# Feed-forward stage: two weight chunks per turn, and later SBUF operands moved to a multiple of 64 bytes

## The reference, cut to what matters

```
# first block: sparse attention mixer (16 heads), then a gated feed-forward layer
h = x + nsa_mixer(rmsnorm(x)) ; h = h + swiglu(rmsnorm(h)) ; x = rmsnorm(h)
def swiglu(h, w_in, w_out):              # D_FF = 5632
    z = h @ w_in                         # 2048 -> 2 * 5632
    a, b = z[..., :D_FF], z[..., D_FF:]
    return (jax.nn.silu(a) * b) @ w_out  # 5632 -> 2048
# second block: mLSTM branch and pooling branch, gated merge, output projection
proj = h @ w_in_2 ; ... ; merged = sigmoid(g_a)*(y_a @ w_a) + sigmoid(g_b)*(y_b @ w_b)
x = x + rmsnorm(merged @ w_out_2)
```

## Time and profile before

| | us |
|---|---|
| median of 3 runs | 2156.36 (2156.34 to 2156.58) |
| the profiled execution | 2156.56 |
| its span | 2154.9 |
| PE busy in it | 2144.7 |
| DVE busy | 1402.0 |
| ACT busy | 1045.4 |

### The profile page before, as it was taken

The page is one execution under the profiler, slowest core; times in us unless marked ns, Lnnn a source line. Parts: engine busy times, 40 slices in busy tenths (PEclk is TensorE's granted clock), DMA queues, the critical chain, the costliest instruction groups (busy, mean ns, idle before and its releaser), DMA issues.

```text
span 2154.9 us, 34222 instructions
## 1 busy us (share of the span) xinstructions
PE 2144.7 (100%) x12210; PEld 1875.6 (87%) x12210; DVE 1402.0 (65%) x1840; ACT 1045.4 (49%) x1371; POOL 68.8 (3%) x145
## 2 busy tenths in 40 slices
PE   9999999999999999999999999999999999999998
PEld 8888889888888888888888888888888888888886
DVE  7766655766666666645556777867777676566564
ACT  6565555544444444434445555444454454444443
POOL 1001221000000000000000000000000000000000
PEclk9999999999999999999999999999999999999999
DMA  8585333555656566565555555545555555555554
GB/s 297 186 271 192 120 128 128 185 186 185 195 169 205 181 196 191 173 200 186 186 185 181 166 169 194 185 158 194 186 176 177 169 191 181 191 188 188 184 200 137
DMA packets 109319, 396.60 MB, mean 184 GB/s; under 512 B 12387, under 2 KB 12403, under 8 KB 109105
## 3 DMA queue, kind: packets, MB, share of 16 engines
q1 hardware_dynamic: 106848, 386.97, 55.3%
q0 software_dynamic: 2240, 8.38, 1.2%
q10 hardware_dynamic: 144, 0.03, 0.0%
HBM read 390.87 MB, written 2.13 MB: 182 GB/s over the span
## 4 chain that ended last, share of the span: by engine, by line
PE 99%; DMA 0%; ACT 0%; POOL 0%; POOLq 0%; issue 0%; SPq 0%
PE set L1534 51%; PE set L1542 26%; PE set L1560 4%; PE set L1566 2%; PE set L1506 2%; PE set L1505 2%; PE set L1504 2%; PE set L1490 1%; PE set L1492 1%; PE set L1491 1%; PE misc L1677 1%; PE set L1648 1%; PE misc L1750 1%; PE misc L1736 1%; PE misc L1897 0%; PE misc L1752 0%
## 5 line engine op out<-in xcount | busy, mean ns | idle before, releaser
L807 DVE TENSOR_TENSOR w_hl<-raw,w_hl 128x1024 fp32r<-128x1024 f32 x729 | 886.6, 1225 | 574.3 <-ACT w_hl L485 568.4
L485 ACT ACTIVATE w_hl<-raw 128x1024 fp32r<-128x1024 f32 x729 | 762.2, 1056 | 798.8 <-PE set L1542 354.7
L1534 PE MATMUL set<-x_hl,w_hl 128*128 128x512 f32 x3520 | 857.2, 393 | 0.0
L1534 PEld LDWEIGHTS set<-x_hl,w_hl 128*128 128x128 f32 x3520 | 644.5, 188 | 124.6 <-issue 0.7
L1542 PEld LDWEIGHTS set<-x_hl,w_hl 128*128 128x128 f32 x3520 | 452.9, 191 | 18.6 <-issue 0.9
L1542 PE MATMUL set<-x_hl,w_hl 128*128 128x256 f32 x3520 | 462.9, 283 | 0.0
L1534 PE MATMUL set<-f_hl,w_hl 128*128 128x512 f32 x704 | 172.7, 396 | 0.0
L1534 PEld LDWEIGHTS set<-f_hl,w_hl 128*128 128x128 f32 x704 | 129.3, 188 | 28.1
L492 ACT ACTIVATE cross<-set 128x512 f32<-128x512 f32 (+1 forms) x142 | 83.2, 586 | 124.2 <-PE set L1534 112.0
L1542 PEld LDWEIGHTS set<-f_hl,w_hl 128*128 128x128 f32 x704 | 90.1, 188 | 4.3
L1560 PE MATMUL set<-w_hl,x_hl 128*128 128x512 f32 x384 | 92.9, 391 | 0.0
(11 more groups left out here) (318 smaller groups left out, 1792.0 us busy)
## 6 DMA issues: line engine op xcount, KB each, us to landing
raw<-in_weights SPq DMA_DIRECT2D x730, 512.0 KB, 4.1
bias_g<-bias POOLq DMA_DIRECT2D x4, 572.0 KB, 3.9
cur<-in_cur POOLq DMA_DIRECT2D x4, 535.0 KB, 3.6
h<-in_x SPq DMA_DIRECT2D x4, 512.0 KB, 7.4
bias<-u_dram POOLq DMA_DIRECT2D x1, 2048.0 KB, 15.0
out<-y_t SPq DMA_DIRECT2D x8, 256.0 KB, 2.4
post_row<-in_post POOLq DMA_DIRECT2D x1, 1024.0 KB, 6.5
w<-in_w POOLq DMA_DIRECT2D x1, 256.0 KB, 4.8
```

The source lines that it names most:

```text
L485: a(high, whole, ACT.Copy).then_inc(hi_ready, 1)
L807: tt(low, whole, high.bitcast(F32), ALU.subtract).then_inc(lo_ready, 1)
L1534: last = mm(out[:, f * 2 * S:(f + 1) * 2 * S], w[:, 0, c], hl[:, kt, :, :], start=first and k == 0, stop=low_first, skip_group_check=True)
```

## The change

In the feed-forward stage (`up` and the down loop) `gemm` gets `paired=True`. The chunks of a unit then run two at a time (`two_chunks`): for the first pair both high groups and then both low groups, for the next pair both low groups and then both high groups, and so on. Of a unit of 11 the last chunk stands alone. `chunks_done` is counted after the second group of each chunk. The wait for `hi_ready` stands in front of every high group now, also in blocks that are not paired. The tensors `f_lead` and `ya_lead` are gone, and `o_lead` (32 bytes) stands ahead of `o_hl`: `o_hl` now starts at byte 180032, `f_hl` and `ya_hl` at 129536, `yb_hl` at 162304, `m_hl` at 178688, all multiples of 64 (and so do the activations and sums that follow them). `x_hl`, `w_hl`, `raw` and `blk_hl` stay where they were. The queues of DVE, ACT, POOL and SP have the same rows in the same order as before.

```diff
@@ sbuf
+            o_lead = sb("o_lead", [P, 8], scope=s1c)
             o_hl = sb("o_hl", [P, HEADS, 2, S], F32R, scope=s1c)
...
-        f_lead = sb("f_lead", [P, 8], scope=s2)
         f_hl = sb("f_hl", [P, FKT, 2, S], F32R, scope=s2)
...
-        ya_lead = sb("ya_lead", [P, 8], scope=s3)
         ya_hl = sb("ya_hl", [P, KT, 2, S], F32R, scope=s3)
...
@@ PE
+        def high_and_low(at, j, out, hl, kts, first, low_first):
...
             def high():
+                pe.wait_ge(hi_ready, at.at(j) + 1)
...
+            return (low, high) if low_first else (high, low)
+
+        def unit_features(at, j, out, hl, kts, first, low_first):
+
+            one, other = high_and_low(at, j, out, hl, kts, first, low_first)
+            one()
+            return other()
+
+        def two_chunks(at, js, k0, out, hl, ready, low_first):
+
+            parts = []
+            for n, j in enumerate(js):
+                kts = range(4 * (k0 + n), 4 * (k0 + n) + 4)
+                parts.append(high_and_low(at, j, out, hl, kts, k0 + n == 0, low_first))
+                if ready:
+                    pe.wait_ge(*ready(kts[-1]))
+                parts[-1][0]()
+            for one, other in parts:
+                other().then_inc(chunks_done, 1)
...
-        def unit(at, j0, number, the_set, n, ready, hl, emit, steps, first_wait=None):
+        def unit(at, j0, number, the_set, n, ready, hl, emit, steps, first_wait=None, paired=False):
...
+            if paired:
+                for j in range(0, n, 2):
+                    two_chunks(at, range(j0 + j, j0 + min(j + 2, n)), j, sets[the_set % 2], hl, ready, j % 4 == 2)
+                    for k in range(j0 + j, j0 + j + 2):
+                        if steps and k in steps:
+                            steps[k]()
+                return
...
@@ def up(i, first)
-                 steps={3: lambda: stats(0, 0, 5)} if first else None)
-            gemm(Pos(C_UP + NB, i, 2 * NB), i * 4 + (B_UP + 2), B_UP)
+                 steps={3: lambda: stats(0, 0, 5)} if first else None, paired=True)
+            gemm(Pos(C_UP + NB, i, 2 * NB), i * 4 + (B_UP + 2), B_UP, paired=True)
...
-                gemm(Pos(C_DOWN + b * ND, i, 2 * ND), i * 4 + (B_DOWN + 2 * b), B_DOWN, n=ND, hl=f_hl,
+                gemm(Pos(C_DOWN + b * ND, i, 2 * ND), i * 4 + (B_DOWN + 2 * b), B_DOWN, n=ND, hl=f_hl, paired=True,
```

More of the change, by code:

```diff
@@ L1523, in block_tokens_apart @@
             return last
-        def unit_features(at, j, out, hl, kts, first, low_first):
+        def high_and_low(at, j, out, hl, kts, first, low_first):
             w = w_hl[at.slot(j)]
@@ L1596, in gemm @@
         def gemm(at, number, the_set, n=NB, ready=None, hl=x_hl, emit=(unit_features, unit_features), steps=None,
-                 first_wait=None):
+                 first_wait=None, paired=False):
             for half in range(2):
                 unit(at, half * (n // 2), number + half, the_set + half, n // 2, ready if half == 0 else None, hl,
-                     emit[half], steps, first_wait if half == 0 else None)
+                     emit[half], steps, first_wait if half == 0 else None, paired)
         def narrow(at, out):
```

## The result

The changed kernel takes 2168.28 us (median of 5 runs, 2168.22 to 2168.47) against 2156.49 for the kernel before: ratio 1.0055, 95% interval 1.0044 to 1.0066, 11.8 us slower. The forecast was 2164.1. The measured time lies 1.3 us above the forecast's own range (2161.5 to 2167) and inside the range given for 8 in 10 (2157.5 to 2170). The profiled span is 2166.7.

What follows compares the result with a forecast made beforehand. PE bounds the kernel, busy throughout with 99% of the chain. Waits +16.0, turns -1.0 and addresses -7.3 sum to +7.7 us on 2156.56, giving 2164.1; own range 2161.5 to 2167, 8 in 10 2157.5 to 2170.

Steps and rivals of the forecast that it cites:

- The waits, +16.0: PE waits for chunk 3's low part: 11 places at 0.96 us, three between down blocks at 1.75; 16.0 us lost.
- T + 7.32: Behind a value block, DVE ends chunk 3's low part 7.32 us after PE starts the next block; PE wants it at 6.51.
- Rival B: Chunk 3's low part comes in time after all, so only the gains stay: -8.3, 2148.1 us; chance 0.06.
- D: Waits longer or more, also at gate-to-value places, or restarts costing 0.3: about +6, 2170 us; chance 0.09.
- the restart: Extra time of PE's matmuls after a wait: 0.05 to start plus 0.10 for the slower second matmul; 0.3 as upper bound.
- The turns, -1.0: Fewer low-to-high turns on PE in `up` and down: 66 saved at 0.015 us, 1.0 us gained.
- The addresses, -7.3: Moved tensors get x_hl's pace: 5.8 us from 152 chunks, 2.0 from m_hl, less 0.5 for narrow o_hl matmuls; 7.3 gained.
- rival A: Tensors' place or what reads beside them, not the address, sets the pace: +15.0, 2171.4 us; chance 0.10.
- Rival C: Aligned f_hl, ya_hl and m_hl run at the bare 0.213 us per 512 columns: 22 us more gained, 2142; chance 0.03.
- The rule on 16-byte lines: Skill page cited against the address gain: crossing 16-byte lines costs, so a 32-byte shift gains nothing and the sum is +15.0.

Runs made afterwards that it cites:

- order_alone: The changed kernel with the old addresses, so only the paired turn order differs from the kernel before: 2171.11 us against 2156.53, ratio 1.0067.
- early_chunk3: The whole change, with ACT and DVE making chunk 3's high and low parts before the work that follows a value or down block: 2153.13 us, ratio 0.9984 to before.
- addr_alone: The kernel before with the change's new addresses and the old order: 2153.18 us, ratio 0.9984.

## Why the prediction was right and where it was not

**The waits, +16.0.** Right in place, number and size, and not by luck: each figure was worked out and each was met. order_alone costs 14.6 where the forecast has 16.0 - 1.0 = 15.0. A gate block takes 23.20 and a value block 22.22, where 23.2 and 22.25 were forecast. The row of the kernel before that gave it is the low part's end at T + 7.32, which could be carried over since nothing between the block end and that part was touched. early_chunk3 took exactly these waits away and 15.2 us with them. Rival B (the part comes in time) is out, and so is D (more or longer waits): no wait shows in value blocks, and the restart cost 0.10, not 0.3.

**The turns, -1.0.** Right in size for x_hl: `up` of early_chunk3 is 490.11 where addr_alone, like before, has 490.77, so 0.7 for 44 turns, and runs of 32 wide matmuls take the 7.28 forecast. Not in down: there the paired order has 247.90 and addr_alone 247.31, 0.6 more rather than 0.3 less. In the trace of early_chunk3 both kinds of f_hl are a little slower than in addr_alone, 233.1 / 119.0 against 232.7 / 118.6, and steps of 229 and 237 ns follow each other in the long runs; why the order does this at that distance is not shown. With the old addresses it did not: the order cost down 253.97 - 248.28 = 5.7 us there and 253.79 - 247.31 = 6.5 with the new ones. These 0.8 cover the 0.6 that is left of the 11.8 when 14.6 and -3.35 are added, 11.2.

**The addresses, -7.3.** This is the term that was mis-sized: -3.35 measured. The step that failed is "I take 7.3 because x_hl is the only aligned tensor in the same role". Alignment to 64 was one of several things in which x_hl differed, and the one that counts is that x_hl and w_hl start at the same place modulo 256, while f_hl moved from 160 to 128 away. One sample of an aligned tensor could not tell these apart, as the prediction said under rival A. The pieces: f_hl 1.0 instead of 3.4; ya_hl 4 x 0.09 = 0.4 instead of 1.2; yb_hl 0.2 instead of 0.6; m_hl 0.1 (its stage is 92.79 us instead of 92.86) and not 2.0. And the o_hl stage, booked as 0.6 for its 16 feature chunks less 0.5 for 384 narrow matmuls, gained 1.5: its narrow pace is 113.7 instead of 118.5, since o_hl came to 192 modulo 256 from w_hl. So 1.5 of the 3.35 came from where the prediction booked nearly nothing, and that part of the gain was luck. Rival A ("the place of the tensors or what reads beside them") was nearer to the cause, but not with its price of nothing. Its full form gave 2171.4; the measured 2168.28 lies between it and the forecast. Rival C (f_hl, ya_hl and m_hl at the bare 0.213) is out: no activation in the table is under 228.6 ns.

**The rule on 16-byte lines** that the prediction took from the Trainium skill (SBUF — State Buffer, section Specifications (TRN2)) says that an access pays when it crosses to a new line. By it the shift of 32 bytes would gain nothing, and neither would one of 64 or 96. The runs differ: eight distances, all multiples of 16 bytes, have chunk times from 2.765 to 2.829 us. So the measurement decides against it as a full account of what a matmul's reads cost.

**The sum.** 14.6 for the order, -3.35 for the addresses and 0.6 for the two together make 11.8, against 16.0 - 1.0 - 7.3 = 7.7. Of the miss of 4.1 the address term is 4.0; the order came out 0.4 cheaper than forecast, and the 0.6 was in no term. The direction was right because the waits are the larger term. The number is outside the forecast's own range because that range gave the addresses at least 6.

## What to carry to other kernels

Before work on a bound engine is regrouped, look at each group that moves forward and ask when its input is ready, measured from the event that starts the chain behind it. A busy share of 100% before says only that the margin was above zero, and here it was 1.0 and 0.3 us, while the order asked for the input 1.8 us earlier. If the input is late only for queue order, move its making ahead of the work that nobody waits for. And when a pace differs between two operands, vary one property at a time, the distance to the other operand included, before pricing "alignment".

## What the runs showed of the hardware that was not expected

The pace of back-to-back float32r matmuls, each with its own weight load, depends on the start addresses of the streamed and the loaded operand in SBUF, by their difference modulo 256 bytes: wide ones from 228.6 to 234.2 ns, narrow ones from 113.8 to 120.1, at a granted clock of 1.00. Only differences in steps of 32 were tried, and 32, 96 and 224 were seen in one run each with the activation streamed; no run here tells by what mechanism. Padding of 64 to 192 bytes between buffers made this kernel 1.0% faster, more than the paired order gave even without its waits (0.7 us in `up`, nothing in down).
